# Scan to output projection without a meeting of the engines, in a diffusion trunk on one NeuronCore

## What is computed

```python
def token_mixing(...):
    ...
    a_l, a_c = mla_mixer(...)
    b_l, b_c = nat_mixer(...)
    c_l, c_c = gdn_mixer(...)
    d_l, d_c = ssm_mixer(...)
    y_lat = jnp.concatenate([a_l, b_l, c_l, d_l], axis=-1) @ w_out
    y_ctx = jnp.concatenate([a_c, b_c, c_c, d_c], axis=-1) @ w_out if need_ctx else None

    # end of gdn_mixer
    def finish(o, zg):
        gate = jax.nn.silu(zg.astype(f32)).reshape(n_b, n_t, GDN_HEADS, GDN_DV)
        return (rms_norm(o, g_norm) * gate).reshape(n_b, n_t, GROUP_W).astype(zg.dtype)

    # end of ssm_mixer
    def finish(y, xs, zg):
        y = (y + xs * d).reshape(n_b, n_t, GROUP_W) * jax.nn.silu(zg.astype(f32))
        y = rms_norm(y.reshape(n_b, n_t, SSM_GROUPS, grp_w), g_norm.reshape(SSM_GROUPS, grp_w))
```

## Time and profile before

| | us |
|---|---|
| median of three executions | 2289.8 |
| lowest, highest | 2284.41, 2292.91 |
| the profiled execution | 2282.64 |
| its span on the trace | 2280.8 |

### The profile page before, as it was taken

How to read it: one execution, slowest core, us unless ns; L and a number is a source line. 1 busy time by engine, 2 the same in 40 slices (tenths; PEclk the granted TensorE clock), 3 DMA queues, 4 the chain that set the end, 5 groups by cost and what they waited for, 6 DMA issues and landing times.

```text
span 2280.8 us, 31525 instructions
## 1 busy us (share of the span) xinstructions
PE 2105.7 (92%) x13261; PEld 1734.4 (76%) x13261; DVE 1087.8 (48%) x1586; ACT 810.0 (36%) x1288; POOL 224.7 (10%) x324
## 2 busy tenths in 40 slices
PE   5999999899988978999999899999979987868997
PEld 4778888687856766788888688888859765767997
DVE  4323333576284565533334633333475557566555
ACT  3322222354345333421223422122344435244343
POOL 0000000100024341000000200000020024420000
PEclk8999999899999989999999899999988999988998
DMA  9464442423224443333423442432332312334662
GB/s 284 129 192 114 125 122 80 147 74 97 74 75 156 161 130 119 86 87 105 109 79 92 120 111 64 126 97 72 119 117 68 121 39 93 112 109 113 176 168 83
DMA packets 403325, 259.07 MB, mean 114 GB/s; under 512 B 21850, under 2 KB 401904, under 8 KB 403184
## 3 DMA queue, kind: packets, MB, share of 16 engines
q1 hardware_dynamic: 403184, 257.06, 38.6%
HBM read 255.97 MB, written 1.05 MB: 113 GB/s over the span
## 4 chain that ended last, share of the span: by engine, by line
PE 80%; DVE 11%; ACT 3%; issue 2%; SPq 1%; POOL 1%; DMA 0%; POOLq 0%; DVEq 0%; ACTq 0%
PE bank L817 23%; PE bank L819 22%; PE bank L818 22%; PE bank L740 2%; PE bank L1164 1%; DVE uT L2012 1%; PE bank L722 1%; DVE wl L1948 1%; ACT wh L1467 1%; DVE mlaw L2267 1%; DVE uT L2010 1%; DVE small L2295 1%; PE bank L761 1%; PE bank L1302 1%; DVE arena L2274 1%
## 5 line engine op out<-in xcount | busy, mean ns | idle before, releaser
L817 PE MATMUL bank<-uh,wh 128*128 128x512 f32 (+1 forms) x1536 | 563.2, 367 | 35.4 <-DVE ul L2018 15.9
L818 PE MATMUL bank<-ul,wh 128*128 128x512 f32 (+1 forms) x1536 | 559.4, 364 | 0.0
L819 PE MATMUL bank<-uh,wl 128*128 128x512 f32 (+1 forms) x1536 | 558.9, 364 | 0.0
L1948 DVE TENSOR_TENSOR wl<-ring,wh 128x2048 fp32r<-128x2048 f32 (+1 forms) x157 | 317.1, 2020 | 171.6 <-ACT wh L1467 170.8
L1467 ACT ACTIVATE wh<-ring 128x2048 fp32r<-128x2048 f32 (+1 forms) x160 | 271.0, 1694 | 316.2 <-PE bank L819 306.1
L817 PEld LDWEIGHTS bank<-uh,wh 128*128 128x128 f32 x1536 | 294.9, 192 | 85.8 <-issue 30.8
L819 PEld LDWEIGHTS bank<-uh,wl 128*128 128x128 f32 x1536 | 294.7, 192 | 44.8
L818 PEld LDWEIGHTS bank<-ul,wh 128*128 128x128 f32 x1536 | 295.0, 192 | 43.5
L817 PE MATMUL bank<-hh,wh 128*128 128x512 f32 (+1 forms) x704 | 255.5, 363 | 1.5 <-DVE wl L1948 1.5
L818 PE MATMUL bank<-hl,wh 128*128 128x512 f32 (+1 forms) x704 | 255.2, 362 | 0.0
L819 PE MATMUL bank<-hh,wl 128*128 128x512 f32 (+1 forms) x704 | 255.2, 362 | 0.0
(11 more groups left out here) (307 smaller groups left out, 2709.8 us busy)
## 6 DMA issues: line engine op xcount, KB each, us to landing
ring<-in_ffn_w_dram SPq DMA_DIRECT2D x176, 512.0 KB, 5.1
ring<-in_w_mod_dram SPq DMA_DIRECT2D x136, 512.0 KB, 4.5
ring<-in_ffn_w_dram SPq DMA_DIRECT2D x64, 384.0 KB, 3.5
ring<-in_ffn_w_dram SPq DMA_DIRECT2D x64, 320.0 KB, 4.1
ring<-in_w_in_dram SPq DMA_DIRECT2D x40, 512.0 KB, 4.7
ring<-in_w_out_dram SPq DMA_DIRECT2D x16, 512.0 KB, 4.5
arena<-in_w_mod_dram SPq DMA_DIRECT2D x8, 512.0 KB, 9.0
ring<-in_w_in_dram SPq DMA_DIRECT2D x4, 544.0 KB, 4.4
```

The source lines that it names most:

```text
L817: pe.matmul(bank, w_hi, x_hi, start=first, stop=False)
L818: pe.matmul(bank, w_hi, x_lo, start=False, stop=False)
L819: return pe.matmul(bank, w_lo, x_hi, start=False, stop=last)
L1948: TT(low[:, b, 0:floats], at, high[:, b, 0:floats].bitcast(F32), ALU.subtract).then_inc(wl_ready, 1)
```

## The change

- The barrier between scan and output projection is gone on all four engines.
- ScalarE takes the first half's roots (in layer 1: loads the Sqrt table) inside step 3, behind the row copy of that step's mod piece.
- In step 3 VectorE makes the last Mamba sums itself, straight from PSUM, and gates them (`last_y`), in place of two copies by ScalarE and `add_y` and `gate_y` by GpSimd. GpSimd scales the first half of layer 0 (`first_scale`).
- VectorE adds the state's part of the DeltaNet output (`add_state`) before it waits for the part within the chunk.
- The first weight piece has buffers of its own, `wh_out` and `wl_out`, over parts of the arena that are free by then. In layer 0 it is rounded behind the roots of the second half, its low part is made behind the scaling. In layer 1 (`early_out`) both happen in step 3, ahead of the last sums, and TensorE does blocks 0 to 3 of outputs 0 and 1 ahead of the transposes.
- `uh` of blocks 0 to 3 is rounded right after the scan and its low parts are all GpSimd's. Blocks 4 to 7 are rounded by ScalarE straight from the transposes' banks, and VectorE makes their low parts from the same banks.
- Some semaphores are merged into counted ones (`params_act`, `gate_dve`, `gate_act`, `roots_set`); the waits keep their order. These hunks are left out below.

```diff
         xdt = uT[:, 6, :].rearrange("p (d n) -> p d n", d=2)
...
             def scan_out(l):
-                mod_work(*mix_mods(l)[3], banks=(0, 2))
-                pe.wait_ge(mod_copied, mix_mods(l)[3][1])
+                mods = mix_mods(l)[3]
+                mod_work(mods.start, mods.stop, banks=(0, 2))
+                pe.wait_ge(mod_copied, mods.stop)
+                pe.wait_ge(sem("y_taken"), outputs_before(l, NT))
+                if early_out(l):
+                    out_blocks(l, (0, 1), range(0, 4))
                 pe.wait_ge(sem("scan_normed"), outputs_before(l, NT) // 2)
                 for b, src in enumerate((o_tm, o_tm, y_tm, y_tm)):
                     for t in tiles_of(halves(l, True)):
@@ -1356,22 +1370,30 @@
                                             src[:, t, (b % 2) * P:(b % 2 + 1) * P], ident)
                     last.then_inc(sem("scan_feature_major"), 1)
 
-            def out_proj(l, hs):
-                t0 = HALF * hs[0]
-                for m in range(KC):
+            def out_blocks(l, ms, ks):
+                t0 = first_out(l)
+                for m in ms:
                     j, b = divmod(m, 2)
                     split = SPLIT[PIECES["out", l][j]]
                     if b == 0:
                         pe.wait_ge(wl_ready, split + 1)
                     pe.wait_ge(y_copied, y_before(l, 1) + m - 1 + Y_CREDIT)
-                    for k in range(KC):
+                    high, low = (wh_out[:, 0], wl_out[:, 0]) if j == 0 else (wh[:, split % 2], wl[:, split % 2])
+                    for k in ks:
                         if m == 0:
-                            wait_low(pe, l, "out", k)
+                            out_low(pe, l, k)
                         ws = slice(k * 256 + b * P, k * 256 + (b + 1) * P)
-                        w_parts = wh[:, split % 2, ws], wl[:, split % 2, ws]
-                        last = split_product(ps[Y_BANKS[b]][:, t0:T], w_parts, (uh[:, k, t0:T], ul[:, k, t0:T]),
-                                             k == 0, k == KC - 1)
-                    last.then_inc(pieces_done if b else y_mixed, 1)
+                        last = split_product(ps[Y_BANKS[b]][:, t0:T], (high[:, ws], low[:, ws]),
+                                             (uh[:, k, t0:T], ul[:, k, t0:T]), k == 0, k == KC - 1)
+                    if KC - 1 in ks:
+                        last.then_inc(pieces_done if b else y_mixed, 1)
+
+            def out_proj(l):
+                if early_out(l):
+                    out_blocks(l, (0, 1), range(4, KC))
+                    out_blocks(l, range(2, KC), range(KC))
+                else:
+                    out_blocks(l, range(KC), range(KC))
 
             def store():
                 for m in range(KC):
@@ -1406,8 +1428,7 @@
                 meet()
                 scan(l)
                 scan_out(l)
-                meet()
-                out_proj(l, post_halves(l, 1))
+                out_proj(l)
...
                     mod_row_out(g, ps[4])
+                    if n == NT - 1:
+                        if len(halves(l, True)) == 2:
+                            finish_roots(l, 0)
+                        else:
+                            load_sqrt()
+                        if early_out(l):
+                            act.wait_ge(sem("sc_ready"), k + 1)
+                            round_out(l)
                     mod_column_out(g, ps[4])
-                    if not state_only(l, n):
+                    if not state_only(l, n) and n < NT - 1:
                         act.wait_ge(sem("ys_ready"), NT * l + n + 1)
                         if k:
                             act.wait_ge(sem("y_added"), 2 * k)
@@ -1848,27 +1877,35 @@
                             A(y_state[:, :, :], ps[7][:, :].rearrange("p (d n) -> p d n", d=2), ACT.Copy)
                         A(tmp_s[:, :, :], ps[6][:, :].rearrange("p (d n) -> p d n", d=2), ACT.Copy
                           ).then_inc(sem("y_taken"), 1)
-                for i, h in enumerate(halves(l, True)):
-                    if i == len(halves(l, True)) - 1:
-                        mod_work(*mix_mods(l)[3], banks=(0, 2))
-                    act.wait_ge(sem("scan_sums"), outputs_before(l, 0) // 2 + i + 1)
-                    o, y = slice(2 * NH * h, 2 * NH * h + 2 * NH), slice(16 + 4 * h, 20 + 4 * h)
-                    A(std[:, o], small[:, 32 + o.start:32 + o.stop], ACT.Sqrt, bias=epsc[:, 0:1], scale=1.0 / 64)
-                    A(std[:, y], small[:, 32 + y.start:32 + y.stop], ACT.Sqrt, bias=epsc[:, 0:1], scale=1.0 / 128
-                      ).then_inc(sem("scan_std"), 1)
-                t0 = HALF * halves(l, True)[0]
+                t0 = first_out(l)
+                for m in range(4):
+                    A(uh[:, m, t0:T], uT[:, m, t0:T], ACT.Copy).then_inc(uh_ready, 1)
+                mods = mix_mods(l)[3]
+                mod_work(mods.start, mods.stop, banks=(0, 2))
+                finish_roots(l, 1)
+                if not early_out(l):
+                    act.wait_ge(sem("ys_ready"), NT * (l + 1))
+                    round_out(l)
                 for b in range(4):
                     act.wait_ge(sem("scan_feature_major"), 4 * l + b + 1)
-                    at = (195, 195, 193, 194)[b]
-                    A(uT[:, 4 + b, t0:T], ps[b][:, t0:T], ACT.Copy, scale=prm[:, l, at:at + 1])
+                    A(uh[:, 4 + b, t0:T], ps[b][:, t0:T], ACT.Copy, scale=prm[:, l, NORM_AT[b]:NORM_AT[b] + 1]
+                      ).then_inc(uh_ready, 1)
+
...
+            def round_out(l):
+                n = PIECES["out", l][0]
+                act.wait_ge(weights_landed[n % RING], 32 * (n // RING + 1))
+                A(wh_out[:, 0, :], ring[:, n % RING, 0:2048], ACT.Copy).then_inc(wh_ready, 1)
 
             def out_proj(l, hs):
-                t0 = HALF * hs[0]
-                for j in range(OUT_PIECES):
+                for j in range(1, OUT_PIECES):
                     round_piece(PIECES["out", l][j], 2048)
-                    if j == 0:
-                        for m in range(KC):
-                            A(uh[:, m, t0:T], uT[:, m, t0:T], ACT.Copy).then_inc(uh_ready, 1)
                     for m in range(2 * j - 4, 2 * j - 2):
                         if m >= 0:
...
-                    elif len(halves(l, True)) == 2:
-                        finish_scale(l, 0)
+                    else:
+                        if len(halves(l, True)) == 2:
+                            finish_inverses(l, 0).then_inc(sem("first_inverses"), 1)
+                        if early_out(l):
+                            split_out(l)
+                        last_y(l, ts)
 
                     if outputs:
+                        add_state(n, ts, [gate(2, d, 0) for d in range(2)])
                         dve.wait_ge(sem("og_ready"), f + 1)
-                        add_out(n, ts, [gate(2, d, 0) for d in range(2)])
+                        add_out(n, ts)
                         if n % 2:
                             dve.wait_ge(sem("o_added"), f + 1)
                 finish_sums(l, 1)
-                finish_scale(l, 1)
+                finish_scale(l)
+                if not early_out(l):
+                    split_out(l)
+                t0 = first_out(l)
+                for b in range(4):
+                    dve.wait_ge(uh_ready, split_before(l, "out") + 4 + b + 1)
+                    STT(ul[:, 4 + b, t0:T], ps[b][:, t0:T], prm[:, l, NORM_AT[b]:NORM_AT[b] + 1],
+                        uh[:, 4 + b, t0:T].bitcast(F32), ALU.mult, ALU.subtract).then_inc(ul_ready, 1)
+
+            def split_out(l):
+                n = PIECES["out", l][0]
+                dve.wait_ge(wh_ready, SPLIT[n] + 1)
+                TT(wl_out[:, 0, :], ring[:, n % RING, 0:2048], wh_out[:, 0, :].bitcast(F32), ALU.subtract
+                   ).then_inc(wl_ready, 1)
+
+            def last_y(l, ts):
+
+                f = outputs_before(l, NT - 1)
+                dve.wait_ge(sem("ys_ready"), NT * (l + 1))
+                dve.wait_ge(sem("y_added"), 2 * f)
+                for d in range(2):
+                    last = TT(heads(y_state[:, d, :]), heads(ps[7][:, d * 256:(d + 1) * 256]),
+                              wide(gates[:, 2, ts[d], d * 8 + 4:d * 8 + 8], 64), ALU.mult)
+                for d in range(2):
+                    y = y_tm[:, ts[d], :]
+                    last = TT(y, y, ps[6][:, d * 256:(d + 1) * 256], ALU.add)
+                last.then_inc(sem("y_taken"), 1)
+                dve.wait_ge(sem("y_taken"), f + 1)
+                for d in range(2):
+                    y = y_tm[:, ts[d], :]
+                    last = TT(y, y, y_state[:, d, :], ALU.add)
+                last.then_inc(sem("y_added"), 2)
+                dve.wait_ge(sem("y_added"), 2 * f + 2)
+                y = y_tm[:, 2:4, :]
+                TT(y, y, zgS[:, 2:4, 0:256], ALU.mult).then_inc(sem("y_gated"), 1)
...
-                link(TT(sq_o, o, o, ALU.mult))
+                dve.wait_ge(sem("y_gated"), i + 1)
```

(49 more changed lines are left out.)

74 lines of the change are left out of this document (40 added, 34 removed).

## The result

| | before | after |
|---|---|---|
| median | 2289.31 us (6 executions) | 2274.04 us (6 executions) |
| lowest, highest | 2284.41, 2292.91 | 2270.74, 2276.66 |
| the profiled execution | 2282.64 (span 2280.8) | 2272.40 (span 2270.5) |

The ratio is 0.9934, interval 0.9922 to 0.9947: 15.3 us or 0.66% less, where 17.4 were forecast.

A forecast was written before the change was run, and what follows sets the result against it. TensorE holds 80% of the chain, so time was to be won where it idles between scan and output projection. Gains of 8.9 (layer 0), 7.6 (layer 1) and 0.9 (scan) make 17.4: 2289.8 to 2272.4 us, range 2262 to 2280.5.

The forecast's parts named there:

- Layer 0: Passage from last scan step to output projection: 8.9 us gained, bounds 7.0 and 11.8, from an earlier start and the clock.
- two meetings, 2.0: Layer 0's last sums: two GpSimd operations meet SBUF-only ones of VectorE, costing 2.0 us, bounds 0 and 2.7.
- 0.53 at 256 columns: Last sums: loss in us of a 256-column SBUF-only VectorE operation that meets GpSimd; about 1.07 at 512 columns.
- the prediction's own sign of being wrong: VectorE's list from last product to sums taking over 11 us, or TensorE waiting again between transposes and projection.
- the 2.3 of which I took half: Layer 0's projection start: 2.3 us lost to low clock before; 1.15 counted as gained, bounds 0 and 2.3.
- Layer 1: Passage from last scan step to output projection: 7.6 us gained, bounds 6.5 and 8.7.
- the new wait: Layer 1, before output 2: TensorE waits for the second weight piece's low part, at 2022.3 where before 2029.9.
- Within the scan: Adding the state's part before the wait for TensorE: 0.3 in step 2 of each layer, 0.3 in layer 0's step 1.
- The clock did not stay up: Rival, chance 0.12: the clock stays up around layer 0's transposes and projection; 22.2 us gained, 2267.6.
- VectorE did become the bound: Rival, chance 0.14: all seven SBUF-only operations of VectorE's last sums meet GpSimd, 5.3 per layer; gain 9.5, 2280.3.
- Nothing landed late: Rival, chance 0.02: layer 1's first weight piece lands late, delaying the last sums; landing at 2030 gives 2303.

The follow-up runs named there:

- e1_before_again: The kernel before, unchanged, timed against itself: 2290.22 us, ratio 1.000.
- the fill: Ten unused matmuls in TensorE's wait ahead of layer 1's input projection: 2266.42 us added to the changed kernel, 2281.55 added to the kernel before.
- e11_low_later: The changed kernel, but in layer 0 GpSimd starts its four low parts only after VectorE's last sums of squares: 2275.01 us, ratio 0.9933 to before.
- e12_low_last: The changed kernel plus ten idle matmuls, with GpSimd's layer 0 low parts held until VectorE's last scaling: 2267.14 us, ratio 0.9904 to before.
- e9_fill_psum: The changed kernel with VectorE's bank-reading last sums first and ten idle matmuls ahead of layer 1's input projection: 2264.26 us, ratio 0.9883 to before.
- e5_psum_first: The changed kernel with VectorE's last sums reordered, those reading a bank ahead of those within work memory: 2265.87 us, ratio 0.9905 to before.
- e3_meet_back: The changed kernel with the four-engine meeting put back ahead of the output projection: 2273.06 us, ratio 0.993 to before.
- e4_no_early: The changed kernel without layer 1's early weight piece and 24 early matmuls: 2274.03 us, ratio 0.9931 to before.
- e2_buffers_only: The kernel before plus only own buffers for the projection's first weight piece, rounded behind the roots: 2274.99 us, ratio 0.9936.

## Why the prediction was right, and where it was not

**Right in the mechanism; that the total came so near is in part luck.** Predicted 2272.4 by a gain of 17.4, measured 2274.04 by 15.3. Against e1_before_again, whose clock in matmuls 9000 to 9850 is like that of after (163.0 and 163.1), the two passages and the stretch behind the second account for 19.3 (9.2, 7.8, 2.3), where 16.5 were predicted, and the spans differ by 18.2. With the fill in both kernels the medians differ by 15.1, and the same stretches by 19.2. So the local sum was rather too low, and some 4 us of it are missing in the medians. In the two filled profiles they lie in stretches that nobody edited: 3.0 in matmuls 9850 to 11300 (23.9 us at half clock against 6.8) and 1.6 in 5250 to 9000 (40.2 against 33.4). The prediction had neither the 2.3 gained behind layer 1's passage nor these losses, and they partly cancel.

**Layer 0: 8.9 predicted, 9.6 measured (against the profile of before), with two errors of opposite sign.** The projection starts 16.4 behind the state's product, predicted 16.0, and 7.4 earlier than before, predicted 7.75. The end of normalisation did not move (837.22 on the axis of before; 836.5 predicted, 837.2 as bound). The term that was mis-sized is "two meetings, 2.0", and with it the price of "0.53 at 256 columns": three operations met GpSimd, the pair L2541 (2.81 instead of 0.80) and the gate (1.65 instead of 0.68), 3.0 in all, about 1.0 for each whatever its columns. The 0.53 came from a row in which GpSimd's instruction, too, had 256 columns; beside such ones, in layer 1, the pair lost 1.0 in all (1.77), near the 1.1 predicted there. That these losses are GpSimd's doing is shown by e11_low_later, where the same two take 0.76 and 0.69. From the first last sum to the roots it was 10.86 us instead of 10.0, 0.14 short of the prediction's own sign of being wrong. Against that the clock gave all of the 2.3 of which I took half: one slow matmul at the start instead of the 4.7 us. In e12_low_last and e9_fill_psum, where the scaling ends 1.6 and 1.4 us sooner behind the first last sum, that slow start comes back; in e5_psum_first, 1.4 sooner as well, it doesn't.

The Trainium skill (GPSIMD Engine Reference, section 1, Specifications) says that GpSimd contends with VectorE's instructions with two SBUF inputs. The traces agree: beside GpSimd the operations with an input from a bank keep their 0.75 (L2532 and L2536 in after), and the pair with two inputs from SBUF takes 2.81 there and 0.76 without GpSimd (e11_low_later).

**Layer 1: 7.6 predicted, 7.9 measured** at the third output: 2022.33 less 0.37 is 2021.96, predicted 2022.3, before 2029.9. Its steps held one by one: weights' low part done at 2003.95 (predicted 2004.1), 24 early matmuls, normalisation ends at 2014.8 (predicted 2015.4), the second piece is the new wait. The row names L2615, a copy of VectorE, as releaser: it stands in VectorE's list behind the low part of the second piece, so it is the same wait, one step longer. What I left out are the 2.3 us behind it: less of matmuls 11500 to 11800 ran at half clock (13.7 us instead of 20.5). In e3_meet_back it is 20.5 again and nothing of the 2.3 is left; e4_no_early keeps 1.3 of them at 20.5, so the clock is not all of it.

The Trainium skill (ScalarE: Activation LUTs, What ACT_TABLE_LOAD costs) counts 2.66 for a change of tables. That is not seen here: the load takes 1.28 at 1998.70, the small root 0.01 behind it, and the gain is not 1.4 less but 0.3 more.

**Within the scan.** Step 2 gained 0.27 (0.3 predicted). Step 1 gained 0.03 instead of 0.3: from one start of the state's product to the next it took 3.44 before and takes 3.41. The second addition of 1.60, taken out of the path, came back in the first:

```profile
796.47 1.11 PE L1283 MATMUL bank<-arena 128*128 128x128 f32 x8
797.19 1.85 DVE L2590 TENSOR_TENSOR arena<-arena 128x256 f32<-128x256 f32 x2
799.88 1.16 PE L1283 MATMUL bank<-arena 128*128 128x128 f32 x8 [2.30 <-DVE arena L2600]
```

GpSimd (L2772, L2777 there) runs on, and whichever addition stands beside it pays.

**The rivals.** The clock did not stay up (0.50 from 838 to 842), and the idle time ahead of the transposes, which this rival saw fall from 3.9 to 3.2, stayed at 3.94. VectorE did become the bound of layer 0's normalisation, but with three operations that met GpSimd and not with seven. (It is the second rival of the list; the prediction's sentence on the two engines calls it the third.) Nothing landed late. The scale on which I took the kernel's scatter, 7.2 between profile and median, held, but I had read it as noise over the whole; most of what parts the two profiles lies in one stage (6.7 us in matmuls 9000 to 9850) and goes with the clock. The range's low end was given as 2262, where 2267.6 less half of the 8.5 us of scatter is 2263.4; nothing hangs on it.

**Still open.** Why the low clock behind the same idle stretch lasts 3.4 us in one execution and 20.5 in another isn't known, nor why e2_buffers_only seems to get off lightly in every execution and the kernel before in few (both by their mean clocks). The fill keeps the clock up there in four profiles of five. Open too are the 3 us by which matmuls 9850 to 11300 differ among kernels that agree in the input projection.

## What to carry to other kernels

Where an edit is worth under one percent, compare the stretch it touches by the order of TensorE's matmuls, and hold or at least read the granted clock of the others: here three kernels that differ by 2.6 to 5.4 us where they were edited had the same median. An idle stretch of TensorE ahead of a stage that is fed block by block can cost more behind it than in it, and a few matmuls of no use may be the cheapest edit of all; in e2_buffers_only, which lost the clock only briefly, they brought nothing. Before moving work to VectorE, list what GpSimd does in the same microseconds, put the operations that read banks there, price each other one by what is left of GpSimd's instruction, and ask what is late next, for the gain ends where the next cover begins.

## What the hardware showed unexpectedly

- Ten matmuls of 512 columns (2.56 us) in an idle stretch of 2.7 us shortened the kernel by 7.6 us. With them the granted clock is 1.00 from 1676 to 1692 at 4.3 to 4.5 us of matmuls in 8; in the trace of after it is 0.50 from 1684 to 1692, where TensorE is busy for 7.66 of 8.
- Behind the same idle stretch of 2.67 us, without those ten matmuls, the clock was low for 3.4, 6.8 or 20.5 us, the first and the last in two executions of one kernel.
- GpSimd beside VectorE: a pair of 256-column additions takes 2.81 instead of 0.76, one of 512 columns 1.65 to 1.75 instead of 0.68, a 2048-column one 3.35 instead of 2.29; GpSimd's four low parts take 5.35, and 7.05 beside the 2048-column one. The loss follows GpSimd's instruction: an operation of VectorE of 16 columns took 1.10 instead of 0.17.
